# Natural projections of a hybrid decoder trunk: two weight slabs on an x that arrives transposed, with the norm's scale applied at PSUM

## The chip, the cores and the metric

One Trainium2 chip, one of its cores. The metric is the device time of one execution in microseconds (us), the median of several runs. TensorE (PE) multiplies, VectorE (DVE), ScalarE (ACT) and GpSimd (POOL) work elementwise, SyncE (SP) issues the DMAs here. Each engine takes its instructions strictly in the order in which they are written; semaphores alone tie the engines together.

## The reference, cut to what matters

```python
def hybrid_layer(x, ...):                       # x: (1, 1024, 1024) float32
    h = rmsnorm(x, norm_w) @ w_in               # y = x * rsqrt(mean(x*x, -1) + 1e-6) * norm_w
    (qa, ka, va, ga, qb, kb, vb, gb, qc, kc, vc, ks, vs, kw, vw, gl, gc) = split(h, ...)
    ...                                         # three attention mixers side by side, gated
    return x + concatenate([ya, yb, yc]) @ w_out
```

The columns of `h` are used in two layouts. Values (`va`, `vb`, `vs`, `vw`) and gate logits (`gl`) are wanted with tokens on partitions: these are the "natural" projections. Everything else is wanted with features on partitions: the "features", 23 chunks of 128 columns.

## The kernel before, in words

The program is a sequence of phases, each a block with its own written list of instructions for every engine: `start_phase`, `diff_phase`, `swa_phase`, `nsa_phase`, `out_phase`. Only `start_phase` changes in substance. There is no scheduler: the order is the order of the code.

All products are made from split operands. A float32 tensor is stored as a high part (a cast to fp32r) and a low part (tensor minus high part), and a product is three matmuls: high by high, high by low, low by high. So a tile of 128 tokens against a slab of weights takes 8 contraction steps (`k`) of three matmuls, 24 in all.

`start_phase` before: x comes in 8 tiles of 128 tokens (`xin`, 4 buffers). For tile i ACT takes the sum of squares and its root (`root`, L363 and L365), DVE makes rstd by four one-column instructions and scales the tile by rstd and the norm's row (`scale_x`, L455 to L462), PE transposes it by 8 matmuls against the identity into PSUM (`turn`, L601), ACT casts it out as `xh` (`x_high_part`, L359) and DVE writes the rest as `xl` (`x_low_part`, L448). Three slabs of weights (256, 256 and 192 columns used) are split by ACT (L372) and DVE (L467). PE runs `natural(n)` (L622 to L624), slab by slab, 24 tiles into four PSUM banks (`nat`). ACT takes the f16 first part of each (`first_part`, L385) and DVE the rest (`value_rest`, L495), which frees the bank; gate logits are copied (L499). The scale of the f16 parts comes from the greatest weight of each slab (`size_slab`, `scale_values`, L473 to L485). Then PE makes feature chunks 0 to 6 (`features(c)`, L637 to L639), each from a 512 KB chunk that ACT and DVE split (L378, L489), in two halves of 24 matmuls of 512 columns; the phase's small "compress" network (L652) lies within them. POOL does two small subtractions at the end of the phase (L591).

## Time and profile before

| what | value |
|---|---|
| median of 3 runs | 835.95 us (832.48 to 838.37) |
| the profiled execution | 829.88 us |
| its span in the trace | 828.1 us |
| lies around the span | 1.78 us |
| PE busy over the span | 758.2 us (92%) |
| DVE, ACT, POOL busy | 554.9, 422.0, 159.9 us |
| granted TensorE clock, mean | 0.969 |

The profiled execution is 6.1 us below the median of the runs shown. Busy time of PE counts matmuls that overlap each other in the pipeline, so the distance between the starts of two matmuls, not the length of one, says what a matmul costs.

### The profile page before, as it was taken

Reading aid. Unit: us, or ns where it says so; the run is one execution under the profiler, and the core shown is the slowest. Engines: PE = TensorE matmul, PEld = TensorE weight load, DVE = VectorE, ACT = ScalarE, POOL = GpSimd, SP = SyncE. Lnnn points to the kernel's source line nnn. Section 1 sums busy time; section 2 is a strip of 40 time slices with the busy share of each in tenths; the row PEclk is TensorE's granted clock in tenths of the full one; section 3 lists DMA queues with packets and bytes.
Section 4 is the critical chain, followed back from the end, with each engine's and each line's share of the span. In section 5 each row is a group of like instructions: output and inputs, shape, how many; then the busy total and the mean of one; then the engine's idle time right before and its main releaser. Section 6 shows DMA issues by size and latency. Waiting matters only on the chain. (4 is left out here: it accounts for less than half of the span.)

```text
span 828.1 us, 16085 instructions
## 1 busy us (share of the span) xinstructions
PE 758.2 (92%) x6224; PEld 654.0 (79%) x6224; DVE 554.9 (67%) x1301; ACT 422.0 (51%) x973; POOL 159.9 (19%) x107
## 2 busy tenths in 40 slices
PE   4899999898988898958998999898999999899996
PEld 3899988677777777746787888787999999788885
DVE  6971111027799998965773998699999999843332
ACT  5631111113557565634762333388999999832121
POOL 0000000002000000001114333253447544232220
PEclk9999999999999999969999999899999999999998
DMA  8302032634141422118115431230001111034431
GB/s 305 110 22 108 26 102 96 158 89 136 47 140 51 129 62 80 51 42 207 40 52 158 128 102 65 79 80 1 3 2 53 52 54 53 2 127 153 152 102 51
DMA packets 31643, 71.81 MB, mean 87 GB/s; under 512 B 5072, under 2 KB 13648, under 8 KB 30544
## 3 DMA queue, kind: packets, MB, share of 16 engines
q1 hardware_dynamic: 31568, 70.78, 27.8%
q8 instruction: 50, 0.82, 0.4%
q14 instruction: 25, 0.20, 0.1%
HBM read 54.52 MB, written 16.25 MB: 85 GB/s over the span
## 5 line engine op out<-in xcount | busy, mean ns | idle before, releaser
L1632 ACT ACTIVATE n_probs<-n_probs,n_negated_max 128x640 f32<-128x640 f32 (+7 forms) x128 | 94.9, 742 | 20.0 <-DVE n_negated_max L1692 19.0
L1701 DVE SCALAR_TENSOR_TENSOR n_probsT_low<-n_turned,n_probsT_high 128x512 f16<-128x512 f32 (+3 forms) x192 | 94.4, 520 | 14.0 <-ACT n_probsT_high L1642 11.7
L708 PE MATMUL n_turned<-identity,n_probs 128*128 128x128 f32 x528 | 80.2, 276 | 4.1 <-ACT n_probs L1632 3.3
L1642 ACT ACTIVATE n_probsT_high<-n_turned 128x512 f16<-128x512 f32 (+3 forms) x192 | 81.0, 457 | 2.4 <-PE n_turned L708 1.8
L1836 PE MATMUL n_scores<-w_and_keys_high,stacks 128*128 128x256 f32 (+2 forms) x192 | 74.6, 388 | 3.0 <-DVE n_negated_max L1692 1.8
L708 PEld LDWEIGHTS n_turned<-identity,n_probs 128*128 128x128 f32 x528 | 60.3, 140 | 13.1 <-ACT n_probs L1632 9.9
L1837 PE MATMUL n_scores<-w_and_keys_low,stacks 128*128 128x256 f32 (+2 forms) x192 | 61.8, 332 | 0.0
L164 POOL TENSOR_TENSOR w_and_keys_low<-w_raw,w_and_keys_high 128x1024 fp32r<-128x1024 f32 x7 | 17.5, 2499 | 220.3 <-ACT w_and_keys_high L149 220.0
L622 PE MATMUL nat<-stacks,xT_high 128*128 128x256 f32 (+1 forms) x192 | 56.2, 293 | 2.3 <-issue 2.2
L623 PE MATMUL nat<-stacks,xT_high 128*128 128x256 f32 (+1 forms) x192 | 55.2, 288 | 0.0
L624 PE MATMUL nat<-stacks,xT_low 128*128 128x256 f32 (+1 forms) x192 | 55.2, 287 | 0.0
L837 ACT ACTIVATE a_probsT_high<-a_turned 128x512 f16<-128x512 f32 (+3 forms) x48 | 21.8, 489 | 61.8 <-PE a_turned L708 61.8
L180 PE MATMUL a_projected<-xT_high,w_and_keys_high 128*128 128x512 f32 x128 | 51.1, 399 | 0.7 <-ACT staged L189 0.7
L2032 PE MATMUL o_acc<-stacks,o_yT_high 128*128 128x512 f32 x128 | 50.4, 394 | 0.2 <-POOL o_yT_low L2005 0.2
L181 PE MATMUL a_projected<-xT_low,w_and_keys_high 128*128 128x512 f32 x128 | 50.5, 395 | 0.0
L182 PE MATMUL a_projected<-xT_high,w_and_keys_low 128*128 128x512 f32 x128 | 50.5, 395 | 0.0
L827 ACT ACTIVATE branches_b_c<-branches_b_c,a_negated_max 128x1024 f32<-128x1024 f32 (+7 forms) x64 | 49.4, 775 | 0.9 <-DVE a_negated_max L895 0.9
L2034 PE MATMUL o_acc<-stacks,o_yT_low 128*128 128x512 f32 x128 | 49.9, 390 | 0.0
L2033 PE MATMUL o_acc<-w_out_low,o_yT_high 128*128 128x512 f32 x128 | 49.9, 389 | 0.0
L895 DVE CUSTOM_DVE_ANT_0 branches_b_c<-a_scores,bias_full 128x1024 f32<-128x1024 f32 (+7 forms) x64 | 47.0, 753 | 0.9 <-PE a_scores L970 0.6
L970 PE MATMUL a_scores<-stacks 96*128 96x512 f32 (+2 forms) x96 | 30.4, 398 | 15.6 <-DVE a_negated_max L895 14.1
L637 PE MATMUL x_transposed<-xT_high,w_and_keys_high 128*128 128x512 f32 x112 | 44.0, 393 | 0.0
(262 smaller groups left out, 2185.4 us busy)
## 6 DMA issues: line engine op xcount, KB each, us to landing
w_raw<-in_w_feat SPq DMA_DIRECT2D x23, 512.0 KB, 3.9
features<-staged SPq DMA_DIRECT2D x30, 256.0 KB, 2.6
a_raw<-features SPq DMA_DIRECT2D x36, 128.0 KB, 2.7
...
branches_b_c<-in_x SPq DMA_DIRECT2D x8, 512.0 KB, 6.3
...
gatesT<-silu_gates SPq DMA_DIRECT2D x8, 512.0 KB, 5.0
...
```

The source lines that it names most:

```text
L180: self.nc.tensor.matmul(bank[:, :], a, self.xh[:, k, cols], start=(k == 0), stop=False)
L181: self.nc.tensor.matmul(bank[:, :], a, self.xl[:, k, cols], start=False, stop=False)
L182: mm = self.nc.tensor.matmul(bank[:, :], b, self.xh[:, k, cols], start=False, stop=(k == KT - 1))
L622: nc.tensor.matmul(nat[n % 4][:, 0:cols], xh[:, k, part], a[:, k, 0:cols], start=(k == 0), stop=False)
L623: nc.tensor.matmul(nat[n % 4][:, 0:cols], xh[:, k, part], b[:, k, 0:cols], start=False, stop=False)
L624: mm = nc.tensor.matmul(nat[n % 4][:, 0:cols], xl[:, k, part], a[:, k, 0:cols], start=False, stop=(k == KT - 1))
L708: mm = nc.tensor.transpose(dst[:, j, :], src[:, c:c + P], ident[:, :])
L1632: nc.scalar.activation(pr[:, n % PS, 0:w], pr[:, n % PS, 0:w], ACT.Exp, scale=-1.0, bias=nmax[:, hb % 4, qt:qt + 1], accum_out=sums[:, hb ...
L1642: nc.scalar.activation(pth[:, g % GS, 0:k, :], tp[g % TS][:, 0:k, :], ACT.Copy, scale=PSCALE).then_inc(t_high, 1)
L1701: nc.vector.scalar_tensor_tensor(out=ptl[:, g % GS, 0:k, :], in0=tp[g % TS][:, 0:k, :], scalar=PSCALE, in1=pth[:, g % GS, 0:k, :], op0=ALU ...
L1836: nc.tensor.matmul(out, q, kh[br][:, keys], start=True, stop=False)
L1837: mm = nc.tensor.matmul(out, q, kl[br][:, keys], start=False, stop=True)
```

## The change

- x is given a second time, transposed by the layout in memory (`x_turned`, 8 tiles of 512 KB). The transposes on PE, the scaled copy of x and the norm's row go away. x in its own layout is still loaded, for the sums of squares, into two buffers.
- POOL multiplies each turned tile by the norm's column (`weigh`), ACT and DVE split it, and PE projects this x without rstd. rstd goes into the scale with which PSUM is read: one number a token, times the value scale (`value_scale`).
- The three slabs become two, of 256 and of 408 columns (128 of vb, 128 of vs, 128 of vw, 24 of gl). PE runs 16 tiles in the order `TILES`: (0,0), (0,1), (1,0), (1,1), then (0,i), (1,i) for i from 2. The first slab's parts lie in the buffers of the feature chunks (`ring.hi`, `ring.lo`).
- The features need the normalised x with features on partitions. rstd is made into a row on all partitions by a matmul of ones with a diagonal (`spread_rstd`), copied by ACT (`copy_rstd`), and POOL multiplies the turned tile by it in place (`normalise`). ACT and DVE then split that tile a second time, over the first split (`normed_high_part`, `normed_low_part`).
- A turned tile has four buffers (`XS`), and tile i from 4 on is loaded after `normed_low_part(i - 4)`.
- The phases behind differ only in which semaphores they use.

The order on POOL in the start phase. Its whole list for this phase before (the first rows are constants):

```order
L2171 MEMSET const-bfloat16-1.0 128x1
L2171 MEMSET const-uint8-127 128x1
L586 UNCONDITIONAL_BRANCH [waits barrier_Pool_Activation_PE_DVE_SP_gather]
L591 ISA
L591 TENSOR_TENSOR stacks<-branches_b_c,stacks 32x1024 [waits a0_stack_high] x2
```

And now, where `branches_b_c` holds the turned tiles, L659 is `weigh` and L665 `normalise`, from `weigh(3)` on:

```order
L659 TENSOR_TENSOR branches_b_c<-branches_b_c,norm_column 128x1024 [waits x_turned_in3]
L665 TENSOR_TENSOR branches_b_c<-branches_b_c,staged 128x1024 [waits x_low_written,rstd_copied]
L659 TENSOR_TENSOR branches_b_c<-branches_b_c,norm_column 128x1024 [waits x_turned_in0]
L665 TENSOR_TENSOR branches_b_c<-branches_b_c,staged 128x1024 [waits x_low_written,rstd_copied]
L659 TENSOR_TENSOR branches_b_c<-branches_b_c,norm_column 128x1024 [waits x_turned_in1]
L665 TENSOR_TENSOR branches_b_c<-branches_b_c,staged 128x1024 [waits x_low_written,rstd_copied]
```

POOL had nothing to do for the projections, and now two operations of 1024 elements a tile stand in one list in turn: `weigh(i + 4)` ahead of `normalise(i + 1)`.

The order on ACT in the middle of the natural projections. Before (L359 the high part of x, L363 and L365 the root, L385 the first parts):

```order
L363 ACTIVATE branch_a,x_square_sums<-branches_b_c 128x1024 [waits x_in1]
L365 ACTIVATE x_rstd<-x_square_sums,norm_eps 128x1 [waits squares_then_roots]
L385 ACTIVATE values_a<-nat1,value_scales_and_inverses 128x4x64 [waits nat_done]
L359 CAST xT_high<-x_transposed0 128x4x128 [waits x_turned]
L359 CAST xT_high<-x_transposed1 128x4x128 [waits x_turned]
```

Now, from `x_high_part(3)` to `first_part(0, 3)` (L387 `x_high_part`, L392 `normed_high_part`, L424 `first_part`, L405 `copy_rstd`):

```order
L387 CAST xT_high<-branches_b_c 128x8x128 [waits x_weighted]
L424 ACTIVATE values_a<-nat0,value_scale_and_rstd 128x4x64 [waits v_scale_and_rstd_set,nat_done]
L396 ACTIVATE branch_a,x_square_sums<-branches_b_c 128x1024 [waits x_in1]
L398 ACTIVATE x_rstd<-x_square_sums,norm_eps 128x1 [waits squares_then_roots]
L392 CAST xT_high<-branches_b_c 128x8x128 [waits nat_done,x_normed]
L424 ACTIVATE values_b_and_selected<-nat1,value_scale_and_rstd 128x4x64 [waits v_scale_and_rstd_set,nat_done]
L424 ACTIVATE values_window<-nat1,value_scale_and_rstd 128x2x64
L405 COPY staged<-features0 128x128 [waits x_normed,rstd_spread]
L387 CAST xT_high<-branches_b_c 128x8x128 [waits x_weighted]
L424 ACTIVATE values_a<-nat2,value_scale_and_rstd 128x4x64 [waits v_scale_and_rstd_set,nat_done]
```

A cast that waits for `normalise(1)` (`x_normed`) now stands in this list ahead of the cast of tile 4 that PE needs.

The order on DVE from `x_low_part(4)` on, now (L496 `x_low_part`, L537 `value_scale`, L548 `value_rest`, L500 `normed_low_part`, then the rstd of tile 4):

```order
L496 TENSOR_TENSOR xT_low<-branches_b_c,xT_high 128x8x128 [waits x_high_written]
L537 TENSOR_SCALAR value_scale_and_rstd<-value_scales_and_inverses,x_rstd 128x1
L537 TENSOR_SCALAR value_scale_and_rstd<-value_scales_and_inverses,x_rstd 128x2
L548 SCALAR_TENSOR_TENSOR values_a<-nat,value_scale_and_rstd,values_a 128x4x64 [waits v_first_part]
L500 TENSOR_TENSOR xT_low<-branches_b_c,xT_high 128x8x128 [waits x_normed_high]
L505 TENSOR_SCALAR x_mean_squares<-x_square_sums 128x1 [waits squares_then_roots]
```

The second split of a tile stands behind the first split of a tile three further on.

The diff, cut to its core:

```diff
+    WA, WB = 4 * HD, 6 * HD + 3 * C_H
+    VW_AT, GL_AT = 4 * HD, 6 * HD
+    SLABS, NV = 2, 3
...
-        wr = sb("slab_raw", [P, 4, KT * P])
-        w1s = wr[:, :, :].rearrange("p a n -> p (a n)").rearrange("p (v l n) -> p v l n", v=2, l=CPL)
+        wr = sb("slab_raw", [P, KT * (WA + WB)])
+        raws = [by_k(wr[:, 0:KT * WA]), by_k(wr[:, KT * WA:])]
+        highs = [by_k(ring.hi[:, :, :, :].rearrange("p a k n -> p (a k n)")), by_k(flat(stacks[:, 0:4, :])[:, 0:KT * WB])]
+        lows = [by_k(ring.lo[:, :, :, :].rearrange("p a k n -> p (a k n)")), by_k(flat(stacks[:, 4:8, :])[:, 0:KT * WB])]
...
+            def load_turned(i):
+                if i >= XS:
+                    sp.wait_ge(n_low, i + 1 - XS)
+                sp.dma_start(turned(i), x_turned[i]).then_inc(xt_in[i % XS], 16)
...
+            load_turned(0)
+            sp.dma_start(ncol[:, :], norm_col).then_inc(rows_in, 16)
+            sp.dma_start(ident[:, :], identity).then_inc(rows_in, 16)
+            load_slab(0, 0)
+            load_slab(0, 1)
+            load_turned(1)
+            load_slab(1, 0)
+            load_slab(1, 1)
             load_x(0)
-            sp.dma_start(nw, norm_row.partition_broadcast(P)).then_inc(rows_in, 16)
-            sp.dma_start(ident[:, :], identity).then_inc(rows_in, 16)
+            load_turned(2)
             load_x(1)
-            load_slab(0)
+            load_turned(3)
+            load_chunk(0)
             load_x(2)
             load_x(3)
-            load_slab(1)
             for i in range(XS, NT):
                 load_x(i)
-            load_slab(2)
-            load_chunk(0)
-            sp.dma_start(w2ks[:, :], w2k).then_inc(consts_in, 16)
-            sp.dma_start(w2vs[:, :], w2v).then_inc(consts_in, 16)
...
-            sp.wait_ge(low, NV)
-            sp.wait_ge(w_sized, NV)
...
             def x_high_part(i):
-                for h in range(2):
-                    act.wait_ge(turned, 2 * i + h + 1)
-                    nc.scalar.copy(xh[:, 4 * h:4 * h + 4, i * P:(i + 1) * P], bank(i, h)).then_inc(x_high, 1)
+                act.wait_ge(weighted, i + 1)
+                nc.scalar.copy(columns(xh, i), turned(i)).then_inc(x_high, 1)
+
+            def normed_high_part(i):
+                act.wait_ge(normed, i + 1)
+                act.wait_ge(done, place(1, i) + 1)
+                nc.scalar.copy(columns(xh, i), turned(i)).then_inc(n_high, 1)
...
+            def copy_rstd(i):
+                act.wait_ge(r_spread, i + 1)
+                if i >= 2:
+                    act.wait_ge(normed, i - 1)
+                nc.scalar.copy(rstd_row[i % 2], rstd_spread[i % 2]).then_inc(r_copied, 1)
...
+            def first_part(s, i):
+                q = place(s, i)
+                act.wait_ge(done, q + 1)
+                act.wait_ge(rv_set, q + 1)
+                for v, at, out in value_parts(s, i, 0):
+                    nc.scalar.activation(out, by_head(nat[q % 4], at, out.shape[1]), ACT.Copy,
+                                         scale=rv[:, i, v:v + 1]).then_inc(v_first, 1)
...
+            split(0, 1)
+            x_high_part(1)
+            split(1, 0)
+            split(1, 1)
             root(0)
+            first_part(0, 0)
+            x_high_part(2)
             root(1)
-            for i in range(NT):
-                x_high_part(i)
-                if i == 0:
-                    split(0)
-                if i == 2:
-                    split(1)
-                if i + 2 < NT:
-                    root(i + 2)
-                if i >= 2:
-                    first_part(i - 2)
-            first_part(NT - 2)
-            first_part(NT - 1)
-            split(2)
-            split_chunk(0)
-            for n in range(NT, NV * NT):
-                first_part(n)
+            first_part(0, 1)
+            copy_rstd(0)
+            first_part(1, 0)
+            root(2)
+            copy_rstd(1)
+            first_part(1, 1)
+            normed_high_part(0)
+            for i in range(2, NT):
+                if i + 1 < NT:
+                    x_high_part(i + 1)
+                first_part(0, i)
+                if i + 1 < NT:
+                    root(i + 1)
+                normed_high_part(i - 1)
+                if i == NT - 1:
+                    split_chunk(0)
+                first_part(1, i)
+                copy_rstd(i)
+            normed_high_part(NT - 1)
 
...
+            def normed_low_part(i):
+                dve.wait_ge(n_high, i + 1)
+                nc.vector.tensor_tensor(columns(xl, i), turned(i), columns(xh, i).bitcast(F32), ALU.subtract).then_inc(n_low, 1)
...
+            def value_scale(s, i):
+                parts = slice(0, 1) if s == 0 else slice(1, 3)
+                nc.vector.tensor_scalar(rv[:, i, parts], vscale[:, 0, parts], rs[:, i:i + 1], None, ALU.mult).then_inc(rv_set, 1)
...
+            def value_rest(s, i):
+                q = place(s, i)
+                dve.wait_ge(v_first, firsts(q + 1))
+                for (v, at, rest), (_, _, high_part) in zip(value_parts(s, i, 1), value_parts(s, i, 0)):
+                    ins = nc.vector.scalar_tensor_tensor(out=rest, in0=by_head(nat[q % 4], at, rest.shape[1]),
+                                                         scalar=rv[:, i, v:v + 1], in1=high_part, op0=ALU.mult, op1=ALU.subtract)
+                if s == 1:
+                    ins = nc.vector.tensor_scalar(glog[:, i, :], nat[q % 4][:, GL_AT:WB], rs[:, i:i + 1], None, ALU.mult)
+                ins.then_inc(freed, 1)
...
-                    size_slab(1)
-                if i >= 2:
...
-            split(2)
-            size_slab(2)
-            split_chunk(0)
+                    x_low_part(i + 1)
+                value_scale(0, i)
+                value_scale(1, i)
+                value_rest(0, i)
+                normed_low_part(i - 2)
+                if i + 1 < NT:
+                    rstd(i + 1)
+                else:
+                    normed_low_part(NT - 2)
+                    split_chunk(0)
+                value_rest(1, i)
+            normed_low_part(NT - 1)
...
+            def weigh(i):
+                pool.wait_ge(xt_in[i % XS], 16 * (i // XS + 1))
+                if i == 0:
+                    pool.wait_ge(rows_in, 32)
+                nc.gpsimd.tensor_tensor(turned(i), turned(i), ncol[:, :].unsqueeze(2).broadcast_to([P, KT, P]),
+                                        ALU.mult).then_inc(weighted, 1)
+
+            def normalise(i):
+                pool.wait_ge(r_copied, i + 1)
+                pool.wait_ge(x_low, i + 1)
+                nc.gpsimd.tensor_tensor(turned(i), turned(i), rstd_row[i % 2].unsqueeze(1).broadcast_to([P, KT, P]),
+                                        ALU.mult).then_inc(normed, 1)
+
+            for i in range(XS):
+                weigh(i)
+            for i in range(NT):
+                normalise(i)
+                if i + XS < NT:
+                    weigh(i + XS)
             for j in range(1, 4, 2):
...
+            def natural(s, i):
+                q = place(s, i)
+                out = nat[q % 4][:, 0:(WA, WB)[s]]
+                a, b = highs[s], lows[s]
+                pe.wait_ge(x_low, i + 1)
+                if q >= 4:
+                    pe.wait_ge(freed, q - 3)
+                xa, xb = columns(xh, i), columns(xl, i)
...
-            for i in range(NT):
-                if i + 1 < NT:
...
                     pe.wait_ge(zeroed, 5)
-                if i == 3:
+                    spread_size(NV, 1)
+                    spread_size(0, 2)
+                if (s, i) == (1, 1):
+                    spread_rstd(0)
                     pe.wait_ge(v_scaled, 1)
-                natural(i)
-                if i == 1:
-                    spread_size(0)
-            spread_size(1)
-            for s in range(1, NV):
-                pe.wait_ge(low, s + 1)
-                for i in range(NT):
-                    natural(s * NT + i)
-                    if (s, i) == (1, 3):
-                        spread_size(2)
-            pe.wait_ge(v_scaled, NV)
+                    spread_size(1, 3)
+                    spread_size(2, 4)
+                    spread_rstd(1)
+                if s == 1 and i >= 2:
+                    spread_rstd(i)
```

## Rows read from the trace of the kernel before

**Rows 1.** The page: span, and PE's busy line.

```profile
span 828.1 us, 16085 instructions
PE 758.2 (92%) x6224; PEld 654.0 (79%) x6224; DVE 554.9 (67%) x1301; ACT 422.0 (51%) x973; POOL 159.9 (19%) x107
```

**Rows 2.** Busy time by stretch: us, then each engine's busy us (instructions), clock, DMA.

```profile
0.00:16.00 16.00, 3.92 (x17) 3.18 (x17) 8.01 (x20) 9.76 (x17) 0.20 (x4) 1.00 0.87 336
16.00:97.00 81.00, 78.20 (x631) 77.56 (x632) 46.32 (x98) 27.13 (x53) 0.00 (x0) 0.98 0.20 73
97.00:180.00 83.00, 80.78 (x331) 63.87 (x331) 14.70 (x21) 11.43 (x16) 0.00 (x0) 0.98 0.36 107
100.00:120.00 20.00, 20.00 (x90) 16.57 (x89) 2.61 (x3) 3.25 (x4) 0.00 (x0) 1.00 0.27 93
```

**Rows 3.** Timeline of PE: start us, length us, what [idle before <-releaser].

```profile
28.87 0.28 PE L623 MATMUL nat<-stacks,xT_high 128*128 128x256 f32 x1
28.99 0.28 PE L624 MATMUL nat<-stacks,xT_low 128*128 128x256 f32 x1
31.49 1.69 PE L601 MATMUL x_transposed<-identity,branches_b_c 128*128 128x128 f32 x8 [2.21 <-DVE branches_b_c L462]
...
33.19 0.41 PE L623 MATMUL nat<-stacks,xT_high 128*128 128x256 f32 x1
33.40 0.41 PE L624 MATMUL nat<-stacks,xT_low 128*128 128x256 f32 x1
...
96.92 0.41 PE L637 MATMUL x_transposed<-xT_high,w_and_keys_high 128*128 128x512 f32 x1
```

**Rows 4.** Groups by form, 0 to 185 us: xcount | busy us, mean ns | idle before.

```profile
L489 DVE TENSOR_TENSOR w_and_keys_low<-w_raw,w_and_keys_high 128x1024 fp32r<-128x1024 f32 x7 | 8.6, 1225 | 6.0 <-ACT w_and_keys_high L378 6.0
L378 ACT CAST w_and_keys_high<-w_raw 128x1024 fp32r<-128x1024 f32 x7 | 7.4, 1052 | 27.8 <-PE x_transposed L639 19.6 <-DMA w_raw<-in_w_feat 8.1
L385 ACT ACTIVATE values_a<-nat,alue_scales_and_inverses 128x256 f16<-128x256 f32 x8 | 3.8, 472 | 4.9 <-PE nat L624 4.3 <-DVE alue_scales_and_inverses L485 0.6
L385 ACT ACTIVATE values_window<-nat,alue_scales_and_inverses 128x128 f16<-128x128 f32 x8 | 2.9, 368 | 18.4 <-PE nat L624 18.4
L495 DVE SCALAR_TENSOR_TENSOR values_a<-nat,alue_scales_and_inverses,values_a 128x256 f16<-128x256 f32 x8 | 3.8, 479 | 3.9 <-ACT values_a L385 3.9
L363 ACT ACTIVATE branch_a<-branches_b_c 128x1024 f32<-128x1024 f32 x8 | 8.5, 1067 | 4.5 <-DMA branches_b_c<-in_x 4.5
L473 DVE TENSOR_REDUCE slab_and_norm_max<-slab_raw 128x1 f32<-128x2048 f32 x2 | 4.6, 2278 | 0.0
L476 DVE TENSOR_SCALAR slab_max_diagonal<-identity,slab_and_norm_max 128x128 f32<-128x128 f32 x3 | 0.9, 288 | 0.1
L458 DVE SCALAR_TENSOR_TENSOR x_newton<-x_rstd,x_mean_squares 128x1 f32<-128x1 f32 x8 | 1.8, 219 | 0.3
L455 DVE TENSOR_SCALAR x_mean_squares<-x_square_sums 128x1 f32<-128x1 f32 x8 | 1.2, 148 | 6.0 <-DMA identity<-in_identity 5.6 <-ACT branch_a L363 0.4
```

**Rows 5.** POOL's broadcast multiplications by form, whole span.

```profile
L1776 POOL TENSOR_TENSOR branch_a<-branch_a,n_subln 128x2048 f32<-128x2048 f32 x1 | 4.6, 4583 | 0.0
L1771 POOL TENSOR_TENSOR branch_a<-branch_a,n_a_rstd 128x2048 f32<-128x2048 f32 x1 | 3.6, 3627 | 10.5 <-DVE n_a_rstd L1677 10.5
```

**Rows 6.** DMA issues, 0 to 180 us: xcount, KB each, median us from issue to landing.

```profile
w_raw<-in_w_feat SPq DMA_DIRECT2D x8, 512.0 KB, 3.5
```

**Rows 7.** Timeline of DVE and POOL where both work.

```profile
185.92 5.72 POOL L591 TENSOR_TENSOR stacks<-branches_b_c,stacks 32x1024 fp32r<-32x1024 f32 x2 [185.48 <-ACT stacks L417]
...
186.12 6.60 DVE L576 SCALAR_TENSOR_TENSOR stacks<-branches_b_c,stacks 32x1024 fp32r<-32x1024 f32 x2
...
383.87 2.46 POOL L164 TENSOR_TENSOR w_and_keys_low<-w_raw,w_and_keys_high 128x1024 fp32r<-128x1024 f32 x1 [192.23 <-ACT w_and_keys_high L149]
...
384.13 2.22 DVE L1186 TENSOR_SCALAR b_negated_sink<-b_sink 128x4 f32<-128x4 f32 x1
```

375 lines of the change are left out of this document (182 added, 193 removed).

## The prediction, made before the change was run

> **What bounds the kernel now.** Read the page's totals first: PE is busy 92% of the span [rows 1]. Then the stretches of the start phase [rows 2]. Up to 16 us PE waits for the first x and weights. From 16 to 97 us it is busy 78.2 of 81 us with the natural projections and the transposes, and from 97 to 180 us 80.8 of 83 us with features, while DVE and ACT are far from full and POOL does nothing. So here a microsecond of PE work is a microsecond of time, as long as the other engines keep up. The distance of two starts is the price of a matmul: 0.12 us for 256 columns with PE warm, 0.21 us after a gap of 2.2 us [rows 3]. That is PE at its 2.4 GHz and its 1.2 GHz level; the second follows an idle gap. A 512-column matmul costs 20 us / 90 = 0.222 us [rows 2]. The first feature matmul starts at 96.92 us [rows 3]. From there the program is the same and bound by PE, so I ask for one number only: when the features start now.
>
> **PE's work.** The 64 transposes go. 24 tiles become 16: eight of 24 x 0.12 = 2.9 us, and eight of 408 columns. Between 0.12 (256) and 0.222 (512) a straight line gives 0.18 us, so 4.35 us a tile. A pair (0,i), (1,i) is 7.2 us, eight pairs 58 us, against 81 us now. The nine matmuls of 128 columns that spread numbers over partitions add about 0.15 us each at their neighbours. If PE stays the bound this is a gain of some 20 us (a rival, below).
>
> **What must keep up.** Per tile from i = 2 on, ACT has two casts of 1024 elements (1.05 us each), a root (1.07, and by my estimate 0.5 us more for its two small parts), first parts of 256, 256 and 128 elements (0.47, 0.47, 0.37) and a small copy: about 5.3 us. DVE has two subtractions of 1024 (1.22), rests (0.48, 0.48, 0.35), rstd by four instructions of 0.15 to 0.22 with a diagonal (0.29) and two value scales: about 5.3 us [rows 4]. POOL has `weigh` and `normalise`. The nearest rows are its broadcast multiplications of 2048 elements, 3.63 us with the small operand constant along the row and 4.58 us with it repeated; halved, 1.8 and 2.3 us [rows 5]. Each load is under 7.2 us, so by throughput PE would stay the bound. By the written order it does not.
>
> **The ring of four tiles.** Follow tile 4. Its load waits for `normed_low_part(0)`, call the end of that N0. POOL's list then has `weigh(4)`, and only behind it `normalise(1)`, though that has long been ready. ACT's list has `normed_high_part(1)`, which waits for `normalise(1)`, ahead of `first_part(1,2)`, `copy_rstd(2)` and `x_high_part(4)`. DVE's has `x_low_part(4)` ahead of `value_scale(0,3)`, on which `first_part(0,3)` waits, and `normed_low_part(1)` behind `value_rest(0,3)`. The end of `normed_low_part(1)` is N1, and it alone lets tile 5 be loaded. So N0 to N1 is one closed chain, with each step once:
>
> load of 512 KB 3.5 us [rows 6]; weigh 1.8, normalise 2.3 [rows 5]; on ACT the cast 0.95 until the next can start, first parts 0.64, copy of 128 columns 0.3 (a row of such a length is 0.37 in full), cast 1.05; on DVE subtract 1.2, value scale 0.15; ACT first part 0.47; DVE rest 0.4 and subtract 1.22 [rows 4]; seven hand-overs of 0.05. Sum 14.3 us.
>
> PE needs 7.2 us of these 14.3 warm, and 9 to 10 if it starts each pair cold, as after the gap in [rows 3]; it waits either way. The chain runs three times (loads of tiles 5, 6 and 7): 43 us.
>
> **When N0 is.** The first turned tile, the column and the identity have landed at about 6 us, my estimate from the start of PE now at 16. Weigh ends at 7.9, the cast at 9.0. From there DVE's list up to N0 holds: five subtractions of 1024 and a slab's two of 1024 (8.4 us), two of 1632 (3.7), reductions 2.28 + 2.28 + 1.2 (5.8) [rows 4], four diagonals, three rstd and three value scales with their small steps (1.0 + 2.5 + 2.9 + 0.8 for the diagonals of rstd), five `value_scale` (0.8), and rests of two tiles of slab 0 and two of slab 1 and one more (3.1): 29.0 us. To it comes 3.6 us in which DVE waits for ACT, most of it for `root(2)`, which stands on ACT behind `first_part(1,0)`, and that behind DVE's own value scales. N0 = 9.0 + 29.0 + 3.6 = 41.6. PE has then done six tiles and works on (0,3).
>
> **POOL beside DVE.** Two DVE instructions of 32x1024 with two operands in SBUF took 6.6 us beside two POOL ones of 5.7 us, and one of 128x4 took 2.2 us from 0.26 us after a POOL subtract began until its end [rows 7]. The same kind alone is 1.22 us (L489) and 0.15 us (L455) [rows 4]. So a DVE instruction can wait out a whole POOL one. In the closed chain POOL works while DVE has nothing, and this costs nothing. Ahead of N0 it hits: `weigh(1)` to `weigh(3)` fall on the first split of x and the slabs' low parts, and `normalise(0)` on small steps. Bounds: 0, and four POOL instructions in full, 8 us; I take 4. At the end, `normalise(5)` starts when `x_low_part(7)` is about 1 us off and `normalise(6)` stands beside the value scales of tile 7: 1.2 us each, 2.4 (bounds 0 and 4.6).
> The Trainium skill has this as a rule (SBUF — State Buffer, section "SBUF: two separate sides"): the two engines share one pair of ports, taken for a whole instruction, and a DVE instruction with two SBUF inputs or in a two-port mode is shut out meanwhile. The rows agree, and the rule speaks against handing POOL this work; by it the two terms are the 6.4 us just given, without it zero.
>
> **The end.** After N3, load, weigh, normalise, ACT's cast, first parts, copy and cast, and DVE's subtract come once more, 12.0 us, and then PE may start (0,7). Behind it: ACT has a root, `normed_high_part(5)`, `first_part(1,6)`, `copy_rstd(6)`, then waits for `normalise(6)`, casts, and casts chunk 0; DVE's low part of chunk 0 comes out 10.0 us after that start. PE's pair takes 7.2 to 9 us meanwhile, and `copy_rstd(7)` ends at about the same 10 us. The second half of chunk 0 needs the last normalised tile 5.3 us later, and that takes 4.6 (2.3 + 1.05 + 1.22): hidden. It would cost about 1 us if POOL and DVE collide there.
>
> **Sum.** 41.6 + 4 + 3 x 14.3 + 12.0 + 10.0 + 2.4 = 112.9 us for the start of the features, against 96.9: 16 us later. Against the profiled execution, 829.88 + 16 = 846; against the median of the runs, which is 6.1 us above that, 835.95 + 16 = 852 us. About 1% (8.4 us) is what a measurement of this kernel can tell from no change.
>
> **Rivals.**
> 1. No collisions, or a POOL that is quicker than its broadcast rows. Then 16 - 6.4 = 9.6 us later, down to 4 if the load lands in 3 us and POOL saves 0.4 us an operation: 840 to 847. For it: by the chain's order POOL and DVE rarely meet. Against it: [rows 7].
> 2. The ring does not bind and PE does: (0,2) starts at about 30 us, when DVE has set the slabs' sizes and two rstd, and the features at 30 + 6 x 7.35 + 1.5 = 75.6, so 21 us earlier, 815 us, faster than before. It decides this way if the chain is under 7.3 us; I find 14.3, of which the load and POOL's two operations alone are 7.6. For it speaks only that every engine's load per tile is under PE's.
> 3. The chain is there but shorter, 9 to 12 us, say because rows of one engine overlap more than I allow: 3 x 2.3 to 3 x 5 us less, with the other terms as forecast or without collisions: 826 to 840.
> 4. The chain is longer: POOL on in-place operands slower than 2.3 us, or a load that shares the queue with the 2 MB of `w1` and lands at 6 to 9 us, and PE cold into the features. Two more microseconds a round and 3 elsewhere: 860 to 868.
>
> **How the numbers follow.** Forecast (847 to 860) 0.50; rival 1 0.20; rival 2 0.10; rival 3 0.10; rival 4 0.10. Slower by over 1% means above 844.3: the forecast, rival 4 and a third of rival 1, 0.67. Faster by over 1%: rival 2 and a trace of 3, 0.11. Within 1%: 0.22. The range runs from 838 to 862: it leaves out rival 2, most of rival 3 and the upper half of rival 4, 0.2 together.
>
> **What would show it.** In the trace of the changed kernel: `weigh` at 1.8 and `normalise` at 2.3 us; loads of turned tiles 4 to 7 issued some 14 us apart; POOL waiting for DMA between `normalise(0)` and `weigh(4)`; ACT's longest waits before L392, for POOL; PE busy about half of 45 to 100 us and at the lower clock at each pair's head; the first feature matmul at 107 to 119 us, and the rest of the span as long as now. Pairs of natural tiles 7.2 us apart throughout would make rival 2 right and this wrong. A phase behind that differs by more than 2 us would be something that I have not seen.

## The result and the profile after

| what | before | after |
|---|---|---|
| median of 4 runs each | 835.20 us (832.48 to 838.37) | 850.46 us (849.08 to 852.35) |
| the profiled execution | 829.88 us | 849.08 us |
| its span | 828.1 us | 847.3 us |
| first feature matmul | 96.92 us | 110.61 us |

The changed kernel is slower: ratio 1.0183, 95% interval 1.014 to 1.0226. 852 us had been forecast, with the features 16 us later; they start 13.69 us later. By the medians of this table the change costs 15.3 us.

The page of the changed kernel, its span and busy totals:

```profile
span 847.3 us, 15699 instructions
PE 755.9 (89%) x5986; PEld 650.9 (77%) x5986; DVE 563.3 (66%) x1320; ACT 429.0 (51%) x982; POOL 197.3 (23%) x123
```

PE has 238 matmuls fewer and falls from 92% to 89% of a longer span [rows 1]. The start phase, now from 16 to 111 us (in [rows 2] it is 16 to 97), and two stretches of 14 us in its middle; the columns are those of [rows 2]:

```profile
16.00:111.00 95.00, 70.24 (x386) 68.17 (x385) 51.71 (x121) 35.92 (x71) 31.31 (x14) 0.86 0.27 95
...
43.00:57.00 14.00, 7.58 (x43) 7.39 (x42) 4.68 (x13) 4.59 (x9) 4.20 (x2) 0.77 0.66 234
57.00:71.00 14.00, 9.96 (x49) 9.75 (x49) 4.40 (x14) 4.24 (x8) 4.25 (x2) 0.74 0.21 75
```

PE was busy 78 of 81 us of the projections; now it is busy 70 of 95, and in the two stretches of 14 us in the middle 7.6 and 10.0 us, at a mean granted clock of 0.77 and 0.74. No engine is near full there: DVE, ACT and POOL are each busy 4 to 5 of 14 us. That is the picture of a chain, not of a bound engine.

The issues of the turned tiles' loads (L315) and of `w1` (L359) in SP's timeline of the changed kernel:

```profile
42.98 0.33 SPq L315 DMA_DIRECT2D branches_b_c<-in_x_turned  x1
...
44.85 0.36 SPq L359 DMA_DIRECT2D slab_raw<-in_cmp_w x1
...
57.20 0.33 SPq L315 DMA_DIRECT2D branches_b_c<-in_x_turned  x1
...
71.69 0.33 SPq L315 DMA_DIRECT2D branches_b_c<-in_x_turned  x1
...
86.17 0.33 SPq L315 DMA_DIRECT2D branches_b_c<-in_x_turned  x1
```

Three rounds of 14.22, 14.49 and 14.48 us. One of them, from 57.20 to 71.69, in the timelines of POOL, ACT and DVE:

```profile
61.00 1.90 POOL L659 TENSOR_TENSOR branches_b_c<-branches_b_c,norm_column 128x1024 f32<-128x1024 f32 x1 [10.24 <-DMA branches_b_c<-in_x_turned]
62.86 2.40 POOL L665 TENSOR_TENSOR branches_b_c<-branches_b_c,staged 128x1024 f32<-128x1024 f32 x1
...
65.28 1.04 ACT L392 CAST xT_high<-branches_b_c 128x1024 fp32r<-128x1024 f32 x1 [8.40 <-POOL branches_b_c L665]
...
67.00 1.06 ACT L387 CAST xT_high<-branches_b_c 128x1024 fp32r<-128x1024 f32 x1
69.54 0.47 ACT L424 ACTIVATE values_a<-nat,value_scale_and_rstd 128x256 f16<-128x256 f32 x1 [1.48 <-DVE value_scale_and_rstd L537]
...
68.09 1.23 DVE L496 TENSOR_TENSOR xT_low<-branches_b_c,xT_high 128x1024 fp32r<-128x1024 f32 x1 [0.21 <-ACT xT_high L387]
...
70.05 0.48 DVE L548 SCALAR_TENSOR_TENSOR values_a<-nat,value_scale_and_rstd,values_a 128x256 f16<-128x256 f32 x1 [0.47 <-ACT values_a L424]
70.45 1.22 DVE L500 TENSOR_TENSOR xT_low<-branches_b_c,xT_high 128x1024 fp32r<-128x1024 f32 x1
```

Read the starts one after the other: load to `weigh` 3.80, to `normalise` 1.86, to the cast of `normed_high_part` 2.42, to that of `x_high_part` 1.72, to `x_low_part` 1.09, to `first_part` 1.45, to `value_rest` 0.51, to `normed_low_part` 0.40, to the next load 1.24. These nine are the 14.49 us, and they are the steps of the prediction's closed chain in its order. Most of the time each engine waits while another has the tile. POOL's longest waits in the start phase say the same (the view of waits: us in total, times, longest):

```profile
POOL branches_b_c L659 <- DMA branches_b_c<-in_x_turned: 50.2, 6, 12.1
POOL branches_b_c L665 <- ACT staged L405: 20.0, 4, 8.1
```

What PE makes of it (its timeline: a cold start in a round, warm 408-column matmuls, and the end of the phase):

```profile
34.58 0.34 PE L703 MATMUL nat<-stacks,xT_high 128*128 128x408 f32 x1
34.76 0.35 PE L704 MATMUL nat<-stacks,xT_low 128*128 128x408 f32 x1
...
54.88 0.58 PE L702 MATMUL nat<-w_and_keys_high,xT_high 128*128 128x256 f32 x1 [6.42 <-DVE xT_low L496]
55.26 0.41 PE L703 MATMUL nat<-w_and_keys_low,xT_high 128*128 128x256 f32 x1
55.47 0.41 PE L704 MATMUL nat<-w_and_keys_high,xT_low 128*128 128x256 f32 x1
...
104.62 0.54 PE L702 MATMUL nat<-stacks,xT_high 128*128 128x408 f32 x1
...
110.61 0.47 PE L721 MATMUL features<-xT_high,w_and_keys_high 128*128 128x512 f32 x1 [0.85 <-ACT staged L405]
```

After three of the four long gaps (6.42, 4.04 and 6.19 us, before 54.88, 69.38 and 99.34) the 256-column matmuls stand 0.21 us apart from the first on, as after the gap in [rows 3] (the 1.2 GHz level), and so for all 24 of tile (0,7): 99.34 to 104.62, 5.3 us, at a granted clock of 0.50. After the fourth gap, 4.39 us before 83.84, they start 0.12 us apart and only stand 0.21 apart from about 85 us on. The 408-column ones, warm, stand 0.184 us apart. The last wait before the features is for `copy_rstd(7)`.

Where POOL and DVE meet in the start phase (their timelines, four places):

```profile
10.53 2.67 POOL L659 TENSOR_TENSOR branches_b_c<-branches_b_c,norm_column 128x1024 f32<-128x1024 f32 x1 [3.76 <-DMA branches_b_c<-in_x_turned]
11.56 1.73 DVE L521 TENSOR_SCALAR staged<-identity,slab_and_norm_max 128x128 f32<-128x128 f32 x1
...
16.85 5.32 DVE L516 TENSOR_TENSOR stacks<-slab_raw,stacks 128x1632 fp32r<-128x1632 f32 x2
17.11 6.83 POOL L659 TENSOR_TENSOR branches_b_c<-branches_b_c,norm_column 128x1024 f32<-128x1024 f32 x2 [3.90 <-DMA branches_b_c<-in_x_turned]
...
95.86 2.35 POOL L665 TENSOR_TENSOR branches_b_c<-branches_b_c,staged 128x1024 f32<-128x1024 f32 x1 [1.95 <-ACT staged L405]
96.75 2.52 DVE L496 TENSOR_TENSOR xT_low<-branches_b_c,xT_high 128x1024 fp32r<-128x1024 f32 x1 [0.21 <-ACT xT_high L387]
...
103.14 2.37 POOL L665 TENSOR_TENSOR branches_b_c<-branches_b_c,staged 128x1024 f32<-128x1024 f32 x1 [4.94 <-ACT staged L405]
103.75 1.78 DVE L537 TENSOR_SCALAR value_scale_and_rstd<-alue_scales_and_inverses,x_rstd 128x1 f32<-128x1 f32 x2
```

The diagonal L521 takes 0.29 us elsewhere, L496 1.22, the two of L537 0.34. Both sides lose: two `weigh` beside the slab's low parts take 6.83 us in place of 3.8.

**Behind the start phase.** The first DMA of the next block, the load of `bias_full`, in SP's timeline of before and of after:

```profile
198.54 0.33 SPq L792 DMA_DIRECT2D bias_full<-in_dist_full  x1
```

```profile
212.23 0.33 SPq L865 DMA_DIRECT2D bias_full<-in_dist_full  x1
```

13.69 us later, to the hundredth what the features are. The rest of the profiled span is another matter: from the first feature matmul to the end it is 731.2 us before and 736.7 us after, with the same matmuls in it (5580 and 5578 records). In the profiled executions of the twelve kernels below, which share that code, the same stretch is 732.7 to 743.4 us long at a granted clock of 0.96 to 0.97. So the 5 us of the 19 between the two profiled executions lie within what such executions differ by. With the medians in place of the profiled times the stretch is 835.20 - 1.78 - 96.92 = 736.5 us before and 850.46 - 1.78 - 110.61 = 738.1 after. What the change costs is the 13.7 us of the start, and up to 1.6 us more behind it that these runs do not tell from nothing.

### The profile page after: what moved, and what is told of

It is laid out like the page before. It is cut to its first block and busy times, and to the rows that moved or that the text cites. A ratio compares the mean times of both kernels' runs of the same rounds, so it can differ in the third digit from the quotient of the medians.

```text
span 847.3 us, 15699 instructions
## 1 busy us (share of the span) xinstructions
PE 755.9 (89%) x5986; PEld 650.9 (77%) x5986; DVE 563.3 (66%) x1320; ACT 429.0 (51%) x982; POOL 197.3 (23%) x123
## 5 line engine op out<-in xcount | busy, mean ns | idle before, releaser
L782 PEld LDWEIGHTS n_turned<-identity,n_probs 128*128 128x128 f32 x528 | 60.2, 141 | 13.3 <-ACT n_probs L1705 10.1
L702 PE MATMUL nat<-w_and_keys_high,xT_high 128*128 128x256 f32 x64 | 24.0, 375 | 33.2 <-DVE xT_low L496 22.8
L900 ACT ACTIVATE branches_b_c<-branches_b_c,a_negated_max 128x1024 f32<-128x1024 f32 (+7 forms) x64 | 49.4, 775 | 1.3 <-DVE a_negated_max L968 1.3
L968 DVE CUSTOM_DVE_ANT_0 branches_b_c<-a_scores,bias_full 128x1024 f32<-128x1024 f32 (+7 forms) x64 | 47.1, 753 | 0.5 <-PE a_scores L1043 0.2
L721 PE MATMUL features<-xT_high,w_and_keys_high 128*128 128x512 f32 x112 | 44.1, 394 | 0.8 <-ACT staged L405 0.8
L702 PEld LDWEIGHTS nat<-w_and_keys_high,xT_high 128*128 128x128 f32 x64 | 17.2, 268 | 34.4 <-DVE xT_low L496 24.0
L723 PE MATMUL features<-xT_high,w_and_keys_low 128*128 128x512 f32 x112 | 43.6, 389 | 0.0
```

The costliest lines, as they stand in the source:

```text
L782: mm = nc.tensor.transpose(dst[:, j, :], src[:, c:c + P], ident[:, :])
```

## The experiments

The theory: the ring of four turned tiles is one closed chain through SP, POOL, ACT and DVE, and each round costs the sum of its steps. The rivals: PE or POOL bounds the rounds, or the collisions of POOL and DVE make the loss. All times of the table are from the runs, all starts from the traces. In the last column stands how much later than in the kernel before the load of `bias_full` is issued.

| kernel | median us (runs) | ratio to before, 95% | loads of tiles 4, 5, 6, 7 | features from | next block |
|---|---|---|---|---|---|
| after | 850.46 (4) | 1.0183 (1.0140 to 1.0226) | 42.98, 57.20, 71.69, 86.17 | 110.61 | +13.69 |
| `pool_swap` | 841.55 (7) | 1.0072 (1.0046 to 1.0099) | 47.02, 58.63, 69.86, 81.27 | 101.69 | +4.76 |
| `dve_swap_alone` | 842.28 (10) | 1.0074 (1.0051 to 1.0098) | 43.16, 53.38, 64.23, 74.44 | 101.21 | +4.26 |
| `pool_and_dve_swap` | 839.28 (10) | 1.0036 (1.0006 to 1.0065) | 45.09, 47.84, 58.45, 70.81 | 96.40 | +1.80 |
| `both_swaps_doubled` | 846.28 (1) | - | 46.96, 49.70, 60.68, 74.37 | 106.89 | +13.37 |
| `normalise_doubled` | 868.85 (4) | 1.0392 (1.0353 to 1.0432) | 45.01, 61.84, 78.69, 95.33 | 126.19 | +31.42 |
| `fifth_buffer` | 830.80 (10) | 0.9953 (0.9928 to 0.9978) | 37.24, 44.88, 56.37, 63.09 | 89.32 | -7.67 |
| `normalise_on_dve` | 834.28 (10) | 0.9979 (0.9961 to 0.9997) | 46.12, 48.87, 59.47, 68.96 | 90.81 | -4.85 |
| `normalise_on_dve_fifth` | 827.49 (4) | 0.9880 (0.9846 to 0.9915) | 36.82, 46.21, 52.52, 59.84 | 83.85 | -10.28 |
| `swaps_w1_late` | 836.58 (12) | 1.0003 (0.9979 to 1.0026) | 47.1, 49.4, 60.4, 69.4 | 94.99 | +0.25 |
| `normalise_on_dve_w1_late` | 831.81 (12) | 0.9952 (0.9929 to 0.9975) | 46.6, 48.9, 60.0, 67.3 | 89.14 | -6.27 |
| `fifth_w1_late_tail` | 825.21 (6) | 0.9878 (0.9855 to 0.9901) | 36.8, 46.2, 52.5, 59.8 | 83.70 | -11.67 |
| `after_w1_late` | 852.74 (6) | 1.0213 (1.0182 to 1.0244) | 44.1, 58.5, 72.8, 87.2 | 112.22 | +15.11 |

The kernel before ran beside them at 835.96 (22 runs), 836.41 (19) and 836.3 us (23) in the three batches. Every time differs from before's by what the last column says and 0 to 3.5 us more (3.5 for `both_swaps_doubled`, which ran once, 2.7 at most for the others). So the start phase is where these differ for the most part; why the rest is never shorter than before's is left open.

**`pool_swap`: the written order on POOL.**

```diff
             for i in range(XS):
                 weigh(i)
+            normalise(0)
             for i in range(NT):
-                normalise(i)
+                if i + 1 < NT:
+                    normalise(i + 1)
                 if i + XS < NT:
                     weigh(i + XS)
```

> The changed kernel with POOL's list alone reordered: normalise(i+1) stands ahead of weigh(i+4). Ring theory: normalise and what ACT does behind it leave the closed chain, so a round is load 3.4, weigh 1.85, cast 1.05, subtract 1.2, value scale and first part 0.9, rest 0.4, subtract 1.2 and hand-overs, about 10.1 us in place of 14.4. Loads of tiles 4 to 7 are issued about 10 us apart, and the features start at 93 to 98 us in place of 110.6, near the kernel before (96.9): 833 to 840 us. Rival (it is POOL's work and its collisions with DVE that cost): POOL does the same work, so it stays within 2 us of 850.

The rounds shrink to 11.6, 11.2 and 11.4 us, and 9 us come back. The links are right, but time and features miss the expected 833 to 840 us and 93 to 98 us. The new length is short by 1.3 us a round. The timelines of POOL and DVE in the second round show why:

```profile
62.21 1.90 POOL L659 TENSOR_TENSOR branches_b_c<-branches_b_c,norm_column 128x1024 f32<-128x1024 f32 x1 [7.04 <-DMA branches_b_c<-in_x_turned]
64.07 2.34 POOL L665 TENSOR_TENSOR branches_b_c<-branches_b_c,staged 128x1024 f32<-128x1024 f32 x1
...
65.22 2.27 DVE L496 TENSOR_TENSOR xT_low<-branches_b_c,xT_high 128x1024 fp32r<-128x1024 f32 x1 [4.41 <-ACT xT_high L387]
```

`normalise` now runs beside the `x_low_part` that the chain waits for, and that subtraction takes 2.27 us in place of 1.22 (2.30 and 2.29 in the rounds beside it). The rest of the miss is tile 4, loaded 4.0 us later than in the change. About 1.9 us of it stand in DVE's list before the edit has any effect: the two weight splits met `weigh` more often in this execution (4.05 and 7.03 us, where the change has 2.43 and 5.32, and 1.73 for L521). The other 2.1 us are L508 of `rstd(2)`, which takes 2.35 us at 38.91 beside the `normalise(1)` that now starts at 38.84.

**`dve_swap_alone`: the written order on DVE.** `normed_low_part(i - 1)` in round i in place of `normed_low_part(i - 2)`, POOL's order as in the change.

```diff
-                normed_low_part(i - 2)
+                if i == 2:
+                    normed_low_part(0)
+                normed_low_part(i - 1)
                 if i + 1 < NT:
                     rstd(i + 1)
                 else:
-                    normed_low_part(NT - 2)
                     split_chunk(0)
```

> The changed kernel with DVE's list alone reordered (normed_low_part(i-1) in the place of normed_low_part(i-2)), POOL's as it was. Ring theory: the closed chain keeps load 3.4, weigh 1.9 and normalise 2.35, but of ACT and DVE only the cast 1.05 and the subtract 1.2 plus hand-overs: 10.0 us a round; loads 10 us apart. The rstd steps of DVE fall into the 3.4 us in which POOL waits for the load, so collisions are fewer than with both swaps. Features at 95 to 99 us, 833 to 840 us. Rival (collisions decide, not the chain): like pool_and_dve_swap or worse, small DVE steps of 1.5 us and more in each round.

Rounds of 10.2, 10.9 and 10.2 us, where 10.0 were expected. The features start at 101.21 and the time is 842.3 us, both above the expected 95 to 99 and 833 to 840: behind the last load L508 takes 1.93 us at 84.91 and 1.98 at 93.84, each beside a `normalise`, in place of 0.22. Either order alone is worth 8 to 9 us, each by another link of the same chain.

**`normalise_doubled`: one step of the chain made longer.** POOL does `normalise` twice, once into a scratch buffer (`scratch` and the dots stand for longer expressions; those who wait for `normed` now wait for twice the count).

```diff
+                nc.gpsimd.tensor_tensor(scratch, turned(i), rstd_row[i % 2]...broadcast_to([P, KT, P]), ALU.mult)
+                pool.wait_ge(normed, 2 * i + 1)
                 nc.gpsimd.tensor_tensor(turned(i), turned(i), rstd_row[i % 2]...broadcast_to([P, KT, P]), ALU.mult)
```

> The changed kernel with each POOL normalise done twice, once into scratch (2.3 us more a tile, same order). Ring theory: POOL stands in the closed chain, so each of three rounds and the last leg get 2.3 us longer and normalise(6) at the end too: features 10 to 12 us later, 121 to 123 us, 860 to 863 us; rounds of 16.7 us. Rival (the chain does not run through POOL, whose load is a third of the time): within 3 us of 850.

Rounds of 16.83, 16.85 and 16.64 us: 2.6, 2.4 and 2.2 us more than in the change, on average the 2.4 us of the instruction in full, though POOL is idle most of the time. The total comes out 6 us above the expectation: the first load is 2 us later, and from the load of tile 7 to the features it is 30.86 us in place of 24.44, nearly three of the doubled operation.

**`pool_and_dve_swap`: both orders**, as in the two diffs above.

> As pool_swap, and on DVE normed_low_part(i-1) stands where normed_low_part(i-2) stood, so the buffer of a tile is free one iteration earlier. Ring theory: the chain of a round is then shorter than PE's pair of 7.2 us, PE runs from about 41 us on without long waits, and the features start at 79 to 85 us: 820 to 825 us, faster than before by 1.2 to 2%. Rival (collisions of POOL and DVE cost the time): the second splits now meet weigh and normalise more often, features not before 93 us.

A miss. If the two links had been all, PE would have become the bound. The features start at 96.40, not at 79 to 85, the time is 839.3 us, not 820 to 825, and TensorE idles 4.07 us in front of them. Two things were in the trace: tile 5 is loaded right behind the 2 MB of `w1` and lands 10.5 us after its issue, and DVE's short steps wait out POOL. `both_swaps_doubled`, the runs with `normalise` on DVE and those with `w1` moved tell how much is whose.

**`both_swaps_doubled`: POOL's part in that.** `pool_and_dve_swap` with `normalise` twice.

> As pool_and_dve_swap, with each normalise done twice on POOL (once into scratch). POOL then has 6.7 us of work a tile and DVE's one- and two-input SBUF instructions wait it out. Collision theory: features 10 us or more later than in pool_and_dve_swap (96), since each of some five blocked DVE steps a tile can wait for one more POOL operation. Chain theory alone (normalise is off the closed chain after both swaps): at most 4 us later, at the end only.

The features move by 10.5 us, from 96.40 to 106.89 (one run). That is as the collision theory has it, and far above the 4 us of the chain theory alone. Where they go can be added up. Measured from one `normed_low_part` (L500) to the next, a round of `pool_and_dve_swap` is 8.97 us (69.56 to 78.53, and 78.53 to 87.51), with L508 of rstd at 1.97 in place of 0.22. The round from 73.12 to 85.04 here is 11.92 us, with L508 at 1.97, the diagonal L512 at 2.31 in place of 0.29 and `x_low_part` at 2.13 in place of 1.22. Take the excess off, 1.75 and 4.68 us, and the two rounds are both 7.2 us.

**`fifth_buffer`: the ring.** A fifth buffer for a turned tile, in a half of `branch_a` that is free in this phase; no order is changed.

```diff
-            return by_k(xt[:, i % XS, :])
+            return by_k(flat(ya[:, :, :])[:, D:2 * D]) if i == XS else by_k(xt[:, (i if i < XS else i - XS - 1), :])
...
-                if i >= XS:
-                    sp.wait_ge(n_low, i + 1 - XS)
+                if i > XS:
+                    sp.wait_ge(n_low, i - XS)
```

> The changed kernel with every list as it is, but a fifth buffer for a turned tile (in a free half of branch_a), so tile 4 is loaded at once and tiles 5 to 7 wait for one normed_low_part less. Ring theory: the chain of 14.4 us now carries two tiles, 7.2 us a tile, which is PE's own pace; the features start at 80 to 86 us: 821 to 827 us. Rival (the written order, not the buffers, or POOL's work): POOL's order is untouched and so is its work, so it stays above 843 us.

The largest gain of one edit: 20 us against the change, with features from 89.32, and now faster than the kernel before by 0.5%. A tile's load no longer closes the loop on the tile just in front of it. The expected 821 to 827 us, features from 80 to 86, are missed all the same, by 4 and 3 us. Tile 4 isn't loaded at once: its load stands on SP behind that of x tile 4, which waits for `root(2)`, and is issued at 37.24. And the tiles then come 9.1 us apart (44.88 to 63.09 for two), not 7.2: DVE is busy 13.3 of 14 us from 51 to 65, and `normed_low_part` takes 2.6, 3.1 and 2.6 us beside POOL (42.22, 53.27 and 60.47) in place of 1.22.

**`normalise_on_dve`: no POOL in the second half of the chain.** Both swaps, `normalise` on DVE with the rstd row read from PSUM, `copy_rstd` gone. The diff shows the operation alone. POOL's list is now the eight `weigh`, and DVE's has `normalise(i - 1)` behind `x_low_part(i + 1)` and `normed_low_part(i - 1)` behind `rstd(i + 1)`, so this run changes an engine and an order together.

```diff
             def normalise(i):
-                pool.wait_ge(r_copied, i + 1)
-                pool.wait_ge(x_low, i + 1)
-                nc.gpsimd.tensor_tensor(turned(i), turned(i), rstd_row[i % 2]...broadcast_to([P, KT, P]),
+                dve.wait_ge(r_spread, i + 1)
+                nc.vector.tensor_tensor(turned(i), turned(i), rstd_spread[i % 2]...broadcast_to([P, KT, P]),
                                         ALU.mult).then_inc(normed, 1)
```

> As pool_and_dve_swap, but the second multiplication (normalise) is done by DVE with the rstd row read from PSUM, so ACT's copy of it goes and POOL has only the eight weigh. Collision theory (in pool_and_dve_swap DVE's small rstd steps waited out POOL's operations): those steps are short again, 0.15 to 0.3 us, except where a weigh falls on them; a tile costs DVE about 6.6 us, up to 8.5 with one weigh waited out, PE 7.3. Features start at 80 to 88 us, 819 to 828 us. Rival (what held pool_and_dve_swap was the load of the turned tiles or the order, not collisions): DVE's list is only longer, the features start at 94 us or later and it is no faster than 836.

The steps of rstd are short again, the operation costs DVE 1.21 us where POOL took 2.35 to 2.65, and 5 us come back against `pool_and_dve_swap`. The time, 834.3 us, and the features, 90.81, are still above the expectation (819 to 828 and 80 to 88). POOL waits 25.84 us for tile 4.

**`normalise_on_dve_fifth`**: that kernel and the fifth buffer.

> As normalise_on_dve, with the fifth buffer of fifth_buffer. If PE or DVE is the bound in normalise_on_dve, a buffer more changes nothing: within 2 us of it. If the load of the turned tiles still holds it, this is 3 to 8 us faster.

6.8 us faster, 1.2% below the kernel before. PE is busy 20.00 of 20 us from 50 to 70 us. What is left stands at the end of the phase, and behind it: PE waits 4.16 us for `normalise(7)` and starts the features cold. Its timeline there:

```profile
83.85 0.76 PE L711 MATMUL features<-xT_high,w_and_keys_high 128*128 128x512 f32 x1 [4.16 <-DVE branches_b_c L495]
84.41 0.63 PE L712 MATMUL features<-xT_low,w_and_keys_high 128*128 128x512 f32 x1
84.84 0.63 PE L713 MATMUL features<-xT_high,w_and_keys_low 128*128 128x512 f32 x1
```

Matmuls 0.43 us apart where warm ones stand 0.23 apart, until 89.9 us. The 13.07 us by which the features come earlier than in the kernel before are 10.28 us at the next block; the missing 2.8 us are this.

**The `w1` load.** Three kernels with the 2 MB load, and the two waits ahead of it, behind the load of the last turned tile; a fourth that also changes the end of DVE's list.

```diff
             for i in range(XS, NT):
                 load_x(i)
                 load_turned(i)
...
-                    sp.wait_ge(low, 2 * SLABS)
-                    sp.wait_ge(w_sized, NV + 1)
-                    sp.dma_start(w1s, w1).then_inc(consts_in, 16)
+            sp.wait_ge(low, 2 * SLABS)
+            sp.wait_ge(w_sized, NV + 1)
+            sp.dma_start(w1s, w1).then_inc(consts_in, 16)
             load_chunk(1)
```

> pool_and_dve_swap with one DMA moved on SP's queue: the 2 MB load of w1 (and the two waits ahead of it) stands behind the load of the last turned tile in place of behind that of tile 4; everything else as in pool_and_dve_swap. That kernel measured 839.3 us, features from 96.4 us, and its load of tile 5 took 10.5 us in place of 3.5, behind w1 in the queues. If the miss of pool_and_dve_swap (96.4 where 79 to 85 was expected) was this load for the most part: tile 5 is there 7 us earlier, features from 89 to 91, 832 to 834 us. If it was the rounds' own collisions (VectorE's short rstd steps that wait out a GpSimd operation, and x_low_part beside normalise), tile 5 only waits elsewhere: features from 94 to 96, 837 to 839 us.

> normalise_on_dve (834.3 us, features from 90.8) with the 2 MB load of w1 behind the load of the last turned tile. Its tile 5 landed 10.4 us after its issue, and weigh(5) waited 7.6 us for it. The fifth buffer, which took the same wait away in another manner, brought 6.8 us. If that wait was the w1 load ahead of it: 5 to 7 us faster, 827 to 829 us, features from 84 to 86. If it was the buffer that came free late: 0 to 2 us, 832 to 834 us.

Both fall on the side of the other theory, the second 0.2 us below its range. The features come 1.4 and 1.7 us earlier, where 5 to 7 us would have been the load's; the times, 839.3 to 836.6 us and 834.3 to 831.8 us, have overlapping intervals. The 7.6 us that `weigh(5)` had waited behind `w1` were for the most part hidden. The rounds of `swaps_w1_late` repeat exactly, 8.97 us apart (60.01, 68.98 and 77.96 are the starts of `normalise`), and its timelines of POOL and DVE show what they are made of:

```profile
60.01 2.65 POOL L666 TENSOR_TENSOR branches_b_c<-branches_b_c,staged 128x1024 f32<-128x1024 f32 x1 [2.10 <-ACT staged L405]
64.97 1.91 POOL L660 TENSOR_TENSOR branches_b_c<-branches_b_c,norm_column 128x1024 f32<-128x1024 f32 x1 [2.31 <-DMA branches_b_c<-in_x_turned]
68.98 2.65 POOL L666 TENSOR_TENSOR branches_b_c<-branches_b_c,staged 128x1024 f32<-128x1024 f32 x1 [2.10 <-ACT staged L405]
...
60.33 0.15 DVE L505 TENSOR_SCALAR x_mean_squares<-x_square_sums 128x1 f32<-128x1 f32 x1
60.51 0.16 DVE L507 RECIPROCAL x_rstd<-x_rstd 128x1 f32<-128x1 f32 x1
60.71 1.97 DVE L508 SCALAR_TENSOR_TENSOR x_newton<-x_rstd,x_mean_squares 128x1 f32<-128x1 f32 x1
...
65.05 1.86 DVE L537 TENSOR_SCALAR value_scale_and_rstd<-alue_scales_and_inverses,x_rstd 128x1 f32<-128x1 f32 x2
```

A step of one column that takes 0.22 us alone takes 1.97: it starts inside `normalise` and ends with it (62.68 against 62.66). The value scales that take 0.34 us take 1.86 and end with `weigh` (66.91 against 66.88). Only the first of these hits is in the loop. The loop runs from L500 down DVE's list (rstd, rests, `x_low_part`) to the first of the two L537, and from there through ACT's `first_part`, `root` and cast back to L500. The hit is on the second L537, behind which L500 would have to wait for ACT's cast anyhow. `pool_and_dve_swap` shows it: one round has the hit on L537 and the next has not, and they are 8.97 and 8.98 us.

```profile
69.56 1.23 DVE L500 TENSOR_TENSOR xT_low<-branches_b_c,xT_high 128x1024 fp32r<-128x1024 f32 x1 [1.81 <-ACT xT_high L392]
...
75.42 1.86 DVE L537 TENSOR_SCALAR value_scale_and_rstd<-alue_scales_and_inverses,x_rstd 128x1 f32<-128x1 f32 x2
...
78.53 1.23 DVE L500 TENSOR_TENSOR xT_low<-branches_b_c,xT_high 128x1024 fp32r<-128x1024 f32 x1 [0.86 <-ACT xT_high L392]
...
84.40 0.35 DVE L537 TENSOR_SCALAR value_scale_and_rstd<-alue_scales_and_inverses,x_rstd 128x1 f32<-128x1 f32 x2
...
87.51 1.23 DVE L500 TENSOR_TENSOR xT_low<-branches_b_c,xT_high 128x1024 fp32r<-128x1024 f32 x1 [1.82 <-ACT xT_high L392]
```

So the collisions cost the round 1.75 us, and without them it would be 8.97 - 1.75 = 7.22 us by this sum, PE's pair. With `normalise` on DVE the rounds are PE's: the timeline of DVE in `normalise_on_dve_w1_late` has `x_low_part` 7.32 us apart, where a pair was worked out at 7.2 us, and PE is busy 14.00 of 14 us from 57 to 71 us.

```profile
60.67 1.22 DVE L487 TENSOR_TENSOR xT_low<-branches_b_c,xT_high 128x1024 fp32r<-128x1024 f32 x1
...
67.99 1.22 DVE L487 TENSOR_TENSOR xT_low<-branches_b_c,xT_high 128x1024 fp32r<-128x1024 f32 x1
```

What holds that kernel is ahead of it: tile 4 is only loaded at 46.6 us, and PE is busy 8.45 of 14 us from 43 to 57 us. The fifth buffer has that load at 36.8 us. So its 6.8 us are those of a buffer that came free late, as the second theory had it; with the late `w1` load on both sides, `normalise_on_dve_w1_late` and the next kernel differ by 6.6 us.

> normalise_on_dve_fifth (827.5 us, features from 83.9) with the w1 load behind the last turned tile, and VectorE's normalise(7) ahead of its split of the first feature chunk instead of behind it. In that kernel TensorE is busy throughout from 50 to 70 us and only idles for 4.2 us before the features, for normalise(7). If TensorE bounds the middle, the late load brings 0 to 1 us and the swap the 1.1 us of the split: 825.5 to 827 us, features from 82.0 to 83.5. If the load of tile 5 still counts there: 2 us more, 823.5 to 825.

```diff
                 if i + 1 == NT:
+                    normalise(NT - 1)
                     split_chunk(0)
-                    normalise(NT - 1)
```

825.21 us falls between the two expected ranges and isn't apart from `normalise_on_dve_fifth`: the ratios are 0.9878 and 0.9880. The features start at 83.70 in place of 83.85, not from 82.0 to 83.5, and the wait in front of them has only changed its name: 4.07 us, now for the split of the first chunk (L537), which stands behind `normalise(7)`. Either order has both on DVE in the same 4 us. The next block comes 1.4 us earlier all the same, and that is the clock: after this gap of 4.07 us the 512-column matmuls start 0.23 us apart and stand 0.43 apart only from 85 to 88 us (granted clock 0.50 from 85 to 87). It is the fastest of the kernels, 1.2% below the one before.

> The changed kernel with nothing but the w1 load moved behind the last turned tile: a control. Its tile 5 is issued at 57.2 us, 12 us after w1, when w1 has long landed, so by every theory the rounds stay at 14.2 to 14.5 us and the features at 110.6: 849.5 to 851.5 us, no difference. If it is faster by over 1.5 us, w1 costs something else in the start than its place ahead of tile 5 (the loads of x beside it, or VectorE's reads).

Rounds of 14.4, 14.3 and 14.4 us; no gain. At 852.74 us it is 1.2 us above the expected range. The features are 1.6 us later, 1.1 of it ahead of tile 4's load, where nothing was changed; the intervals of the two ratios overlap.

## Why the prediction was right

Point by point, by the prediction's own terms (us):

| term | forecast | measured |
|---|---|---|
| N0 with the early collisions | 41.6 + 4 = 45.6 | 42.98 (the load it releases) |
| three rounds | 3 x 14.3 = 42.9 | 14.22 + 14.49 + 14.48 = 43.19 |
| last leg, with one collision | 12.0 + 1.2 = 13.2 | 86.17 to 99.34 = 13.17 |
| the end, with one collision | 10.0 + 1.2 = 11.2 | 99.34 to 110.61 = 11.27 |
| features from | 112.9 | 110.61 |

That the time came within 1.6 us of 852 is in part luck: the features are 2.3 us earlier than forecast, and the rest of the medians' difference lies behind them.

- **The ring as a closed chain** carried the sum, and was right link by link. `pool_swap` and `dve_swap_alone` each cut a link by order alone and took 3 and 4 us out of every round. `normalise_doubled` lengthened one and put 2.2 to 2.6 us into every round. `fifth_buffer` opened the loop and removed the loss.
- **N0** is the term that was mis-sized, by 2.6 us. About 1.1 of it is the start: `weigh(0)` starts at 4.87 us where 6 was estimated. The early collisions came to 1.4 (L521) and 1.6 us (L516, 5.32 where 3.7 was forecast), 3.0 in place of 4. The last 0.5 us are spread over DVE's list.
- **Prices**: `weigh` 1.90 (1.8), `normalise` 2.34 to 2.40 (2.3), the 408-column matmul 0.184 (0.18), the load to `weigh` 3.5 to 3.8 (3.5).
- **The end** came out by another path than the one that was costed, so 11.27 for 11.2 is luck. DVE's low part of chunk 0 ends at 109.32, 10.0 us after PE's start with the collision at 103.75 in it, where the forecast had 10.0 without one. The last to come is `copy_rstd(7)` at 110.47, behind PE's cold pair of 99.34 to 109.37; the prediction had it at 10 us after PE's start, and it came at 11.1.
- **Rival 1 (no collisions, 840 to 847)** failed: 3.0 us early and 1.3 us at 96.75 lie on the path. The 1.4 us at 103.75 are in the trace too, but what they delay is done before the features start. The rule of the Trainium skill that was set beside them (SBUF — State Buffer, section "SBUF: two separate sides") gave the right sign; of the 6.4 us set for it 4.3 counted.
- **Rival 2 (PE bounds, 815)** is what the kernel with both reorderings, `normalise` off POOL and a fifth buffer comes nearest to: its rounds are 7.3 us, its features start at 83.7 to 83.9 where the rival had 75.6, and the rest is the late tile 4 and the end.
- **Rivals 3 and 4** (rounds of 9 to 12, rounds longer by 2) are excluded by the rounds themselves; `w1`, a reason given for the fourth, costs the changed kernel nothing that `after_w1_late` can show. The times given for rival 3 don't follow from its own terms: 852 less 6.9 to 15 us, and less 6.4 more without collisions, is 831 to 845 us, not 826 to 840.
- **A phase behind that differs by more than 2 us** does stand in the profiled execution (5.5 us over the rest of the span), while the medians have 1.6 us. Why a given execution has 732 and another 743 us there is left open.
